# The second attention of a two-block kernel, taken by two heads of a token tile at a time

## What is computed

```python
    scores = scores - slopes * absdist.astype(jnp.float32)
    scores = jnp.where(mask[None, :, None, None, :, :], scores, -jnp.inf)
    sink_l = sink.astype(jnp.float32).reshape(N_KV_HEADS, Q_GROUP)[:, :, None, None]
    m = jnp.maximum(jnp.max(scores, axis=-1, keepdims=True), sink_l)
    p = jnp.exp(scores - m)
    denom = jnp.sum(p, axis=-1, keepdims=True) + jnp.exp(sink_l - m)
    p = (p / denom).astype(v.dtype)
    out = jnp.einsum("bnhgqk,bnkhd->bnqhgd", p, vb)
```

## Time and profile before

| | us |
|---|---|
| median of 3 runs | 2061.53 (2061.19 to 2062.84) |
| the profiled execution, its own time | 2061.77 |
| its span, first to last instruction | 2060.0 |
| the stage, first logits to last value product | 1419.4 to 1584.7 |
| PE busy | 1962.3 (95% of the span) |
| DVE, ACT, POOL busy | 887.4, 786.0, 523.1 |

### The profile page before, as it was taken

The page is one execution under the profiler, slowest core; times in us unless marked ns, Lnnn a source line. Parts: engine busy times, 40 slices in busy tenths (PEclk is TensorE's granted clock), DMA queues, the critical chain, the costliest instruction groups (busy, mean ns, idle before and its releaser), DMA issues.

```text
span 2060.0 us, 24487 instructions
## 1 busy us (share of the span) xinstructions
PE 1962.3 (95%) x10404; PEld 1592.9 (77%) x10404; DVE 887.4 (43%) x1446; ACT 786.0 (38%) x1139; POOL 523.1 (25%) x117
## 2 busy tenths in 40 slices
PE   6999988999999999989899999989998999999998
PEld 5887766778777877778788888877666878888886
DVE  2014336676768766543311344342665431103243
ACT  4224544355444543423422322343556242212222
POOL 2422120000000000024243444423222334444442
PEclk8999998999999989999999999999999999999999
DMA  4711121000011000143223222222112222223222
GB/s 146 240 62 62 69 80 33 24 24 21 25 37 30 22 21 31 39 177 123 92 102 103 85 99 102 82 107 67 62 42 82 82 92 102 86 98 103 102 84 80
DMA packets 54513, 160.80 MB, mean 78 GB/s; under 512 B 3295, under 2 KB 30303, under 8 KB 39684
## 3 DMA queue, kind: packets, MB, share of 16 engines
q1 hardware_dynamic: 42476, 135.40, 19.5%
q10 hardware_dynamic: 11928, 23.83, 3.4%
HBM read 152.63 MB, written 10.25 MB: 79 GB/s over the span
## 4 chain that ended last, share of the span: by engine, by line
PE 84%; DVE 8%; ACT 5%; issue 2%; DMA 1%; POOL 0%; SPq 0%; ACTq 0%; DVEq 0%
PE ps L571 22%; PE ps L572 21%; PE ps L573 21%; PE ps L664 2%; PE ps L686 2%; PE ps L908 2%; PE ps L918 2%; PE ps L916 2%; DVE stat L1755 1%; PE ps L678 1%; DMA w_raw<-in_wpack 1%; PE ps L948 1%; PE ps L945 1%; PE ps L996 1%; PE ps L925 1%
## 5 line engine op out<-in xcount | busy, mean ns | idle before, releaser
L562 POOL TENSOR_TENSOR w_lo<-w_raw,w_hi 128x2048 fp32r<-128x2048 f32 x113 | 522.9, 4629 | 1506.7 <-ACT w_hi L1171 1506.6
L571 PE MATMUL ps<-ht_hi,w_hi 128*128 128x512 f32 (+1 forms) x1304 | 531.9, 408 | 15.0 <-DVE ht_lo L1685 8.2
L572 PE MATMUL ps<-ht_lo,w_hi 128*128 128x512 f32 (+1 forms) x1304 | 503.8, 386 | 0.0
L573 PE MATMUL ps<-ht_hi,w_lo 128*128 128x512 f32 (+1 forms) x1304 | 503.8, 386 | 0.0
L1171 ACT ACTIVATE w_hi<-w_raw 128x2048 fp32r<-128x2048 f32 x126 | 241.0, 1914 | 489.6 <-PE ps L573 438.1
L571 PEld LDWEIGHTS ps<-ht_hi,w_hi 128*128 128x128 f32 x1304 | 251.7, 193 | 93.9 <-issue 44.5
L573 PEld LDWEIGHTS ps<-ht_hi,w_lo 128*128 128x128 f32 x1304 | 251.1, 193 | 49.6
L572 PEld LDWEIGHTS ps<-ht_lo,w_hi 128*128 128x128 f32 x1304 | 252.5, 194 | 39.6 <-issue 1.9
L2110 DVE TENSOR_TENSOR hid_lo<-hidden,hid_hi 128x1024 fp32r<-128x1024 f32 x27 | 129.3, 4788 | 149.1 <-ACT hid_hi L1535 149.1
L571 PE MATMUL ps<-w_hi,hid_hi 128*128 128x512 f32 x432 | 168.1, 389 | 0.0
L573 PE MATMUL ps<-w_hi,hid_lo 128*128 128x512 f32 x432 | 168.1, 389 | 0.0
(11 more groups left out here) (258 smaller groups left out, 2719.7 us busy)
## 6 DMA issues: line engine op xcount, KB each, us to landing
w_raw<-in_wpack SPq DMA_DIRECT2D x114, 1024.0 KB, 4.9
w_raw<-in_wpack SPq DMA_DIRECT2D x24, 512.0 KB, 5.3
bias_skewed_dram<-bias_rows_dram ACTq DMA_DIRECT2D x1, 3840.0 KB, 22.8
toe<-bias_skewed_dram ACTq DMA_DIRECT2D x1, 3072.0 KB, 13.0
x_res<-in_x SPq DMA_DIRECT2D x4, 512.0 KB, 6.6
gate_dram<-side_tile ACTq DMA_DIRECT2D x8, 256.0 KB, 2.7
merged<-gate_dram ACTq DMA_DIRECT2D x1, 2048.0 KB, 9.7
gate<-gate_dram ACTq DMA_DIRECT2D x1, 2048.0 KB, 12.2
```

The lines of the kernel that those rows point to most:

```text
L562: nc.gpsimd.tensor_tensor(Wl[:, slot, :], raw[:, slot, :], f32(Wh[:, slot, :]), ALU.subtract).then_inc(lo_ready, 1)
L571: mm(dst, wh, ah, start=first, stop=False)
L572: mm(dst, wh, al, start=False, stop=False)
L573: return mm(dst, wl, ah, start=False, stop=last)
```

## The change

An item is now a pair of heads (2j and 2j+1) of one query tile: 16 items in place of 32. The two heads lie in rows 0 to 63 and 64 to 127 of the same tile of `q2_t`, and their outputs fill all 128 rows of one tile of `att2_out`. The logits of the two heads go to banks 4 and 5, one behind the other. Their transposes keep bank 6 and come one head after the other, and the value products alternate between the two heads, in one block of bank 7. Between two blocks of value products there are still 8 pieces of the gates for every two heads: 3, then 2, then 3.

The logits of both heads lie in one tile whose rows are one longer than before. Column 0 holds the sink, put there by ACT (`put_sink`), so that one reduction gives both maxima with the sink, one instruction negates both, and the sum of the exponential holds the sink's already. L1223, L1750 and L1755 have no successor. There are now two such tiles and two tiles of transposed probabilities; two of the four are laid over tiles of the first block that are no longer used. The output of both heads is copied in one instruction of 128 rows. DVE does two steps of the pooling branch in an item. ACT takes the sigmoid after every second item and splits a weight unit after every second item, at the end of the even ones. The second attention has its own semaphores and its own code; the function that both attentions shared keeps only what the first one uses.

```diff
-        LG2 = r("logits2", [P, 2, 3 * P])
-        PT2 = r("probs_t2", [P, 3, P])
+        LG2 = [r("logits2_even", [P, 2, 3 * P + 1]), place("logits2_odd", [P, 2, 3 * P + 1], at=fwa_at)[0]]
+        PT2 = [r("probs_t2_low", [P, 3, P]), place("probs_t2_high", [P, 3, P], at=oat_at + 4 * 3 * P)[0]]
...
-        items2 = []
-        for h in range(Q_HEADS2):
+
+        pairs2 = []
+        for j in range(Q_HEADS2 // 2):
             for qt in range(NT):
                 lo, hi = max(0, qt - 1), min(NT, qt + 2)
-                rows = slice(HD * (h % 2), HD * (h % 2) + HD)
-                kv = h // 4
+                rows = [slice(HD * h, HD * h + HD) for h in range(2)]
+                kv = j // 2
                 x0 = (lo - (qt - 1)) * P
                 n = (hi - lo) * P
-                items2.append(dict(
-                    segs=[dict(bank=4 + len(items2) % 2, n=n, off=0, q=Q2[rows, h // 2, qt * P:(qt + 1) * P],
-                               k=KD[rows, kv, lo * P:hi * P],
-                               slope=-(2.0 ** -(h + 1)),
-                               bias=AD[:, x0:x0 + n])],
-                    vals=[V2[:, kb, kv * HD:(kv + 1) * HD] for kb in range(lo, hi)], n=n, sink=h, rows=rows,
-                    out=O2[rows, h // 2, qt * P:(qt + 1) * P]))
-        att = [dict(items=items1, LG=LG1, PT=PT1, first=0, banks=(7, 3), out_bank=2, outs=1),
-               dict(items=items2, LG=LG2, PT=PT2, first=len(items1), banks=(6,), out_bank=7, outs=4)]
+                pairs2.append(dict(
+                    n=n, j=j, rows=rows, bias=AD[:, x0:x0 + n], out=O2[:, j, qt * P:(qt + 1) * P],
+                    q=[Q2[rows[h], j, qt * P:(qt + 1) * P] for h in range(2)],
+                    k=[KD[rows[h], kv, lo * P:hi * P] for h in range(2)],
+                    slopes=[-(2.0 ** -(2 * j + h + 1)) for h in range(2)],
+                    vals=[V2[:, kb, kv * HD:(kv + 1) * HD] for kb in range(lo, hi)]))
...
+            def pair_attention(fill):
+
+                def logits(i):
+                    it = pairs2[i]
+                    if i:
+                        pe.wait_ge(a2["read"], i)
+                    for h in range(2):
+                        last = mm(bank(4 + h, it["n"]), it["q"][h], it["k"][h], start=True, stop=True)
+                    last.then_inc(a2["logits"], 1)
+
+                logits(0)
+                for i, it in enumerate(pairs2):
+                    if i + 1 < len(pairs2):
+                        logits(i + 1)
+                    fill(3)
+                    for h in range(2):
+                        pe.wait_ge(a2["probs"], 2 * i + h + 1)
+                        if h:
+                            fill(2)
+                            pe.wait_ge(a2["turned_taken"], 2 * i + 1)
+                        for j in range(len(it["vals"])):
+                            last = nc.tensor.transpose(ps[:, 6, j * P:(j + 1) * P],
+                                                       LG2[i % 2][:, h, 1 + j * P:1 + (j + 1) * P], ident)
+                        last.then_inc(a2["turned"], 1)
+                    fill(3)
+                    pe.wait_ge(a2["turned_taken"], 2 * i + 2)
+                    if i:
+                        pe.wait_ge(a2["out_taken"], i)
+                    for j, v in enumerate(it["vals"]):
+                        for h in range(2):
+                            last = mm(ps[it["rows"][h], 7, 0:P], v, PT2[h][:, j, :],
+                                      start=j == 0, stop=j == len(it["vals"]) - 1)
+                    last.then_inc(a2["out"], 1)
...
-            attention(att[1], lambda slot: advance(gate_work, 2))
+            pair_attention(lambda n: advance(gate_work, n))
             assert next(gate_work, None) is None
-            pe.wait_ge(o_taken, len(items1) + len(items2))
+            pe.wait_ge(a2["out_taken"], len(pairs2))
...
+            def put_sink(i):
+
+                j = pairs2[i]["j"]
+                actf(LG2[i % 2][:, :, 0:1], SNK[:, 2 * j:2 * j + 2].unsqueeze(2), ACT.Copy).then_inc(a2["sink_put"], 1)
+
+            def pair_exponentials(i):
+                act.wait_ge(a2["maxima"], i + 1)
+                st = 16 + 8 * (i % 2)
+                for h in range(2):
+                    row = LG2[i % 2][:, h, 0:pairs2[i]["n"] + 1]
+                    actf(row, row, ACT.Exp, bias=stat[:, st + 2 + h:st + 3 + h],
+                         accum_out=stat[:, st + 4 + h:st + 5 + h]).then_inc(a2["exps"], 1)
+
+            put_sink(0)
+            put_sink(1)
+            pair_exponentials(0)
+            for i, it in enumerate(pairs2):
+                nv = len(it["vals"])
+                for h in range(2):
+                    act.wait_ge(a2["turned"], 2 * i + h + 1)
+                    if i and h == 0:
+                        act.wait_ge(a2["out"], i)
+                    actf(PT2[h][:, 0:nv, :].rearrange("p a b -> p (a b)"), bank(6, nv * P),
+                         ACT.Copy).then_inc(a2["turned_taken"], 1)
+                if i + 1 < len(pairs2):
+                    pair_exponentials(i + 1)
+                if i + 2 < len(pairs2):
+                    put_sink(i + 2)
+                if i % 2:
+                    u = i // 2
                     d = USE0["gatep"] + u
                     dst = MG2[:, 2 * u:2 * u + 2, :] if u < 4 else G2[:, 2 * u - 8:2 * u - 6, :]
                     act.wait_ge(pair_full, d + 1)
                     actf(dst, ps[:, 2 * (d % 2):2 * (d % 2) + 2, :], ACT.Sigmoid).then_inc(pair_taken[d % 2], 1)
-
-            def gate_weights(i):
-                if i % 4 == 1:
-                    hi(UNIT0["gatep"] + i // 4 + 2)
-
-            attention(att[1], take_gate, gate_weights)
+                act.wait_ge(a2["out"], i + 1)
+                actf(it["out"], bank(7, P), ACT.Copy).then_inc(a2["out_taken"], 1)
+                if i % 2 == 0:
+                    hi(UNIT0["gatep"] + i // 2 + 2)
...
-            attention(att[1], lambda i: next(pool_work, None))
+            for i, it in enumerate(pairs2):
+                st, n = 16 + 8 * (i % 2), it["n"]
+                LG = LG2[i % 2]
+                dve.wait_ge(a2["logits"], i + 1)
+                if i >= 2:
+                    dve.wait_ge(a2["turned"], 2 * i - 2)
+                for h in range(2):
+                    ins = v.scalar_tensor_tensor(LG[:, h, 1:n + 1], it["bias"], it["slopes"][h], bank(4 + h, n),
+                                                 ALU.mult, ALU.add)
+                ins.then_inc(a2["read"], 1)
+                dve.wait_ge(a2["read"], i + 1)
+                dve.wait_ge(a2["sink_put"], i + 1)
+                order(v.reduce_max(stat[:, st:st + 2], LG[:, :, 0:n + 1], AX.X))
+                v.tensor_scalar(stat[:, st + 2:st + 4], stat[:, st:st + 2], -1.0, None, ALU.mult).then_inc(a2["maxima"], 1)
+                next(pool_work, None)
+                next(pool_work, None)
+                for h in range(2):
+                    dve.wait_ge(a2["exps"], 2 * i + h + 1)
+                    order(v.reciprocal(stat[:, st + 6 + h:st + 7 + h], stat[:, st + 4 + h:st + 5 + h]))
+                    v.tensor_scalar(LG[:, h, 1:n + 1], LG[:, h, 1:n + 1], stat[:, st + 6 + h:st + 7 + h], None,
+                                    ALU.mult).then_inc(a2["probs"], 1)
```

25 lines of the change are left out of this document (8 added, 17 removed).

## The result

| | before | after |
|---|---|---|
| median, us | 2061.66 (2061.19 to 2062.84) | 2024.05 (2023.27 to 2025.52) |
| span of the profiled execution | 2060.0 | 2021.4 |
| first logits of the stage to the start of its last block of value products | 164.75 | 128.86 |
| the same to the end of that block, as in the earlier trace rows | 165.33 | 129.51 |

What follows compares the result with a forecast made beforehand. PE was taken to bound the stage: 1.52 + 5.79 + 0.55 = 7.86 us a pair against 9.78, 1.92 less, times 16 is 30.7; 2061.8 - 30.7 = 2031 us. Range 2026 to 2041 for 8 in 10.

Steps and rivals of the forecast that it cites:

- Both kinds: Second attention on PE: two heads' logits, and likewise their value products, run at the same time; forecast 2031 us, chance 0.72.
- rivals 1, 2 and 3: Value products or logits in turn (2040/2048 us, 0.11/0.03); small DVE/ACT holds of PE (2034 to 2047, 0.09); POOL blocking PE (2069, 0.04).
- Rival 4: The sink's column costs what it saves; dismissed as unable to move PE, within the forecast's range; no chance of its own.
- The pair: PE's steady work for two heads in the stage: 7.86 us against 9.78, 1.92 less, counted 16 times.
- the 0.10 for issuing eight more instructions: Block of value products and logits for two heads: 1.42 us plus 0.10 to issue the added instructions, 1.52.
- Its start and its end I leave as they are, give or take 2.: Stage's start (wait for the pooling input) and end (sigmoid, copy, next product): unchanged, within 2 us.
- The wait: PE's wait for the scaled row behind POOL's subtraction: expected to go through 1.5 us of cover, saving 0.4 for two items.
- 0.8 a round for the wait: Old kernel, middle of the stage: of 19.56 us a round of four items, products fill 18.7 and the remaining 0.8 is waiting.
- The rule against overlap: Value products of two heads, differing in columns alone: by the skill page they take turns, making the sum 8.8 us worse.
- Distances of 7.7 to 7.9: Sign: starts of successive items' first value products lie 7.7 to 7.9 us apart at a granted clock of 1.00.
- A stage of 134 to 135: Sign: 134 to 135 us from the first logits to the last value product; over 139 would be wrong.
- A blocked negation or pooling step: Sign: POOL's subtraction still stretches one such DVE instruction to up to 4.7 us in each of 8 rounds.

Runs made afterwards that it cites:

- sink_column_alone: Kernel before, still 32 items of one head, with only the sink as column 0 of the logits and without L1223, L1750 and L1755; 2056.41 us.
- start_hold: Changed kernel with one more 1792-element DVE reduction in the first pair only, and one gate piece there moved behind PE's first transposes; 2026.74 us.
- dve_plus_1: Changed kernel with one more 1024-element reduction (1.2 us) on DVE in every second pair from the third on; 2024.47 us.
- negated_apart: Changed kernel with DVE's first logits not waiting for ACT's pooling copies, sink copies first, negation as two one-column instructions, pooling steps behind scalings; 2020.1 us.
- start_early: Changed kernel with DVE taking the first pair's logits without waiting for ACT's pooling copies, and ACT's sink copies put ahead of those; 2027.79 us.

## Why the prediction was right or wrong

**Direction, mechanism and block: right.** Both kinds overlap; rivals 1, 2 and 3 didn't come to pass. Rival 4 was dismissed with a wrong reason, that the sink's small instructions can't move PE: sink_column_alone gained 6.8 us by them. The stage's 36.33 us are, by the same cut for both kernels: from the first pair's value products to the last's 146.89 - 115.29 = 31.60; the start 17.86 - 13.57 = 4.29; the end, to `yp_hi`, 3.48 - 3.04 = 0.44.

**The pair: 2.11 us less, where the sum had 1.92.** 31.60 over 15 distances. The block was taken as 1.52 and is 1.43: the 0.10 for issuing eight more instructions, an allowance without a row of its own, measured 0.01. The gate products lie nearer 0.231 than 0.233 apart. And the last of the distances gave 3.2 (10.20 before, with a wait of 1.27 in it, and 6.98 after), the others 2.03 each. Over 15 distances the miss is 2.8 us.

**The step that failed: "Its start and its end I leave as they are, give or take 2."** In the sum the start stood at 1.92, as any pair; it gave 4.29. The trace of before has a wait of PE there, 1.92 us, with the clock at half speed behind it, and the sum valued neither. Taken alone, the start's 2.4 is just outside the allowance, with the end's 0.4 further. sink_column_alone shows the size: the wait gone, 2.73. An estimate from these rows, that price and a pair's steady gain less its share of the old wait (2.03 - 0.33 = 1.70), makes 4.4 for the 4.29 measured. start_hold shows the other direction, a wait put back, at 4.55 us in its profile and some 2.7 in its median.

All three misses have one sign. Added up, 2.8 + 2.4 + 0.4 = 5.6 us of the 6.9 between forecast and result. The other 1.3 lie outside the stage. Behind it the two profiles differ by 1.9 us (472.38 and 470.48 from `yp_hi` to the end), and the clock was at 0.50 there for 13.4 and 9.3 us, as told above. The sum has no term for this, and whether the change brings it about or it fell so by luck is open.

**The wait: gone, but the reason was half the story.** The prediction said that the longer round would cover the blocked time, and cover of at least 1.2 us is there (dve_plus_1). But sink_column_alone lost most of the waits with the old rounds. The column takes L1755 of the earlier trace rows, the instruction that POOL blocked, out of the chain; the block then falls on the scaling behind it, with nothing left to do after it. This gain of 6.8 would have come without any pairs. The prediction's 0.8 a round for the wait was also too much: PE waits 0.67 to 0.69 in a round of the middle.

**The rule against overlap: not borne out here.** The Trainium skill, "TensorE: Matmul & The Clock Gate", part 3, "What overlaps and what doesn't", says that weight loads run beside products in flight only where the row group differs. From this the prediction took 8.8 us for value products that take turns. That went further than the page, whose sentence is about weight loads. Here two products that differ in columns alone start 0.01 us apart, and six of both heads take 0.81 against 0.80 for three of one head. The Trainium skill, "SBUF — State Buffer", "Who interferes with whom", says that a `tensor_scalar`, and so the scaling, can take the port pair shared with GpSimd. No row of before showed one blocked; sink_column_alone does, 3.08 us, and negated_apart, 1.72, where it otherwise takes 0.35, and the traces agree with the page.

**What would show it.** Distances of 7.7 to 7.9 with a clock of 1.00 were foretold; they are 7.60 to 7.85, 7.73 on average, at 1.00, so half of them lie just below. A stage of 134 to 135: 129.5, shorter by the terms above. A blocked negation or pooling step, harmless: so it is, in seven of the eight rounds.

## What to carry to other kernels

Products of two heads that write different column halves cost one head's time here when their instructions alternated, and so did those that read different row halves, one behind the other. Put them side by side, and don't pay the slow product behind such a block twice. A wait of TensorE (PE) of about 2 us or more cost 1.2 to 1.8 times its length here, and twice its length in one profile, depending on whether and for how long the granted clock fell with it. So the first and last waits of a stage belong in the sum with more than their length, and not into "as before". If GpSimd (POOL) and VectorE (DVE) meet, look at which VectorE instruction starts beside the GpSimd one: in start_early, starting the chain earlier gained nothing while a blockable instruction stood in it. And what stands behind the blocked instruction counts: with the scaling last, the same block cost next to nothing.

## What the hardware showed that I had not expected

A negation of 128x2 was held until GpSimd's subtraction ended (4.29, 4.18, 2.00 us), one of 128x1 was not (0.15), while a maximum of two tensors of 128x1 was (2.59). A reduction over 514 elements ran beside it in its usual 0.69. Three instructions of one head ran ahead before the other head's began, so that blocks of three tiles by head took 1.07 and alternating ones 0.81. And the code ahead of the stage, the same in all kernels of the study, brought the first logits anywhere from 1418.14 to 1424.09, a spread larger than some of the differences in question. Behind the stage such a spread, 4.8 us, went with the time at which the granted clock was at 0.50.
